# Laced conditioning weights as split single passes, and cache rows transposed behind the queries

## The reference

```
mod = silu(c) @ w_ada + b_ada                 # c: two conditioning vectors of 1024; w_ada: 1024 x 6144
sh1, sc1, gt1, sh2, sc2, gt2 = split(mod, 6)
h = x * (1 + sc1) + sh1
z = h @ w_in                                  # cq, ckv, kr, gu, gv
q = rms(cq) @ w_uq;  ckv = rms(ckv);  kr = rope(kr)        # ckv, kr are outputs too
a = chunk_causal_attention(q, ckv_all @ w_uk + kr_all, ckv_all @ w_uv)
b = gelu(gu) * (W_s LN(gelu(gv)) + b_s)       # gMLP; the normalised v rows of the sample are an output
m = [rms(a) * g_a, rms(b) * g_b] @ w_o
x1 = LN(alpha * x + (1 + gt1) * m);  then a product-key expert layer, and x2 = LN(...)
```

## Time and profile before

| | |
|---|---|
| median of 3 runs | 1888.17 us (1888.16 to 1888.47) |
| the profiled execution | 1888.05 us |
| its span in the profile | 1886.2 us |
| TensorE busy | 1747.3 us (93%) |
| VectorE, ScalarE, GpSimd busy | 1439.2, 672.8, 835.0 us |

### The profile page before, as it was taken

The page is one execution under the profiler, slowest core; times in us unless marked ns, Lnnn a source line. Parts: engine busy times, 40 slices in busy tenths (PEclk is TensorE's granted clock), DMA queues, the critical chain, the costliest instruction groups (busy, mean ns, idle before and its releaser), DMA issues.

```text
span 1886.2 us, 28376 instructions
## 1 busy us (share of the span) xinstructions
PE 1747.3 (93%) x9464; PEld 1501.2 (80%) x9464; DVE 1439.2 (76%) x2852; ACT 672.8 (36%) x948; POOL 835.0 (44%) x633
## 2 busy tenths in 40 slices
PE   7799899999699699898799999999999999999995
PEld 1799753486599599788688989989889899898894
DVE  2532614444599999979299998988999999999997
ACT  1223233322222245578333333333333333333333
POOL 1114210010333256678465555545556555555564
PEclk9899979999799899999899999999999999999997
DMA  8122203322321243544899999999999999999992
GB/s 299 57 68 65 87 27 126 112 90 68 111 68 41 82 157 123 221 155 194 336 389 396 371 380 383 371 379 381 370 371 385 380 382 370 384 379 370 384 341 90
DMA packets 144116, 459.41 MB, mean 244 GB/s; under 512 B 13936, under 2 KB 46720, under 8 KB 143136
## 3 DMA queue, kind: packets, MB, share of 16 engines
q1 hardware_dynamic: 85808, 224.42, 33.8%
q0 software_dynamic: 57360, 208.72, 28.8%
q10 hardware_dynamic: 864, 25.17, 3.2%
HBM read 423.31 MB, written 34.68 MB: 243 GB/s over the span
## 4 chain that ended last, share of the span: by engine, by line
PE 82%; DVE 7%; ACT 4%; DMA 3%; POOL 2%; issue 2%; ACTq 0%; DVEq 0%; POOLq 0%; SPq 0%
PE ps L620 81%; ACT piece L1076 2%; POOL e_lo L569 1%; DMA early_activations<-e_out 1%; DMA g_in<-dense_gates 1%; DMA w_raw<-peer_uT 1%; ACT e_hi L1076 1%; DVE tmp L1433 0%; DMA consts_sb<-consts 0%; POOL act_lo L514 0%; DMA gath<-peer_u,idx 0%; DVE stats L1916 0%; POOL w_lo L507 0%; PE ps L868 0%; DVE y_tok L1914 0%
## 5 line engine op out<-in xcount | busy, mean ns | idle before, releaser
L620 PE MATMUL ps<-act_hi,w_hi 128*128 128x384 f32 (+1 forms) x1496 | 480.4, 321 | 46.4 <-POOL w_lo L507 20.3
L620 PE MATMUL ps<-act_hi,w_lo 128*128 128x384 f32 (+1 forms) x1496 | 475.8, 318 | 0.0
L620 PE MATMUL ps<-act_lo,w_hi 128*128 128x384 f32 (+1 forms) x1496 | 475.3, 318 | 0.0
L602 POOL DMA_INDIRECT gath<-peer_v,idx x192 | 259.2, 1350 | 205.1 <-DVE f_full L1827 159.1
L602 POOL DMA_INDIRECT gath<-peer_u,idx x192 | 251.6, 1311 | 209.6 <-DVE act L1822 175.8
L620 PEld LDWEIGHTS ps<-act_hi,w_hi 128*128 128x128 f32 x1496 | 284.6, 190 | 52.4 <-POOL w_lo L507 20.4
L620 PE MATMUL ps<-v_hi,ga_hi 128*128 128x512 f32 x768 | 299.5, 390 | 3.1 <-DVE v_lo L1811 3.1
L620 PE MATMUL ps<-v_hi,ga_lo 128*128 128x512 f32 x768 | 301.2, 392 | 0.0
L620 PE MATMUL ps<-v_lo,ga_hi 128*128 128x512 f32 x768 | 301.2, 392 | 0.0
L620 PEld LDWEIGHTS ps<-act_lo,w_hi 128*128 128x128 f32 x1496 | 284.5, 190 | 4.2
L620 PEld LDWEIGHTS ps<-act_hi,w_lo 128*128 128x128 f32 x1496 | 284.2, 190 | 0.0
(11 more groups left out here) (268 smaller groups left out, 2725.7 us busy)
## 6 DMA issues: line engine op xcount, KB each, us to landing
w_raw<-peer_uT SPq DMA_DIRECT2D x128, 512.0 KB, 6.9
v_raw<-peer_v SPq DMA_DIRECT2D x96, 512.0 KB, 7.7
w_raw<-ada SPq DMA_DIRECT2D x48, 512.0 KB, 3.5
dense_gates<-piece ACTq DMA_DIRECT2D x6, 4096.0 KB, 11.8
g_in<-dense_gates SPq DMA_DIRECT2D x32, 768.0 KB, 14.3
w_raw<-peer_v SPq DMA_DIRECT2D x32, 512.0 KB, 7.1
w_raw<-w_in SPq DMA_DIRECT2D x17, 512.0 KB, 3.3
w_raw<-w_pq SPq DMA_DIRECT2D x16, 512.0 KB, 3.6
```

What stands on the lines that cost most here:

```text
L602: pool.indirect_dma_start(out=gath[:, u % GB, :], out_offset=None, in_=table, in_offset=bass.IndirectOffsetOnAxis(ap=idx12[:, par, u:u + 1 ...
L620: return nc.tensor.matmul(out, lhsT, rhs, start=start, stop=stop)
```

## The change

The 24 laced slots are split like the other weights: ACT writes the high part of slot x to `w_hi[x % 2]` (`ada_high`), GpSimd the low part to `w_lo[x % 2]` (`ada_low`). The condition is split too, into four columns `silu_hl` (high part of two vectors, low part of two). A piece is then two single passes, `silu_hl` with the high and with the low part of the weights, which sum into four rows of PSUM; VectorE adds the two pairs of columns in `conditioning`. The transposes of the cache rows move from behind the gMLP product to behind the swap of q's rope halves, ahead of w_uk, in banks 2 and 3; `o_tok` moves to the region of the probabilities, and `new_v` is sent behind its DMAs. Four of the eight pieces ahead of the loop move in front of the token sums. The semaphores `vmean` and `vvar` are merged into `rowsA`, which makes room for `ahi` and `alo`. The places of the new buffers:

```
+        silu_hl = at("silu_hl", [P, KD, 4], R["small"] + 1024, F32R)
...
-        o_tok = at("o_tok", [P, NT, KVL + ROPE], R["rows"])
+        o_tok = at("o_tok", [P, NT, KVL + ROPE], R["p"])
...
+        def ada_slot(x):
+            r = RING_AT["ada2"] + x
+            return r % RING, 16 * (r // RING + 1)
+        N_LACED = 4 * len(LACED)
+        A0 = FIRST["ada2"]
```

GpSimd, behind the output DMAs:

```
-            low_mix(0, GH)
+            def ada_low(x):
+                pool.wait_ge(s["ahi"], x + 2)
+                nc.gpsimd.tensor_tensor(w_lo[:, x % 2], w_raw[:, ada_slot(x)[0]], w_hi[:, x % 2].bitcast(F32),
+                                        ALU.subtract).then_inc(s["alo"], 1)
+            for x in range(7):
+                ada_low(x)
+            low_mix(0, 2)
+            for x in range(7, 9):
+                ada_low(x)
+            low_mix(2, GH)
+            for x in range(9, N_LACED):
+                ada_low(x)
```

TensorE: `ada_piece`, then the transposes behind the swap of q's rope halves (the same lines, with banks 6 and 7, are removed from behind the gMLP product), then the order ahead of the units, where the token sums stand behind the wait for `sqb`:

```
                 j, i = divmod(n, 2)
+                x = 4 * (g - LACED[0]) + j
                 if i == 0:
-                    pe.wait_ge(s_w[r % RING], 16 * (r // RING + 1))
-                ins = mm(ps[0:2, 7, :], silu_c[:, n, :], w_raw[:, r % RING, i * 512:(i + 1) * 512], n == 0, n == 7)
+                    pe.wait_ge(s["alo"], x + 1)
+                c = slice(i * 512, (i + 1) * 512)
+                mm(ps[0:4, 7, :], silu_hl[:, n, :], w_hi[:, x % 2, c], n == 0, False)
+                ins = mm(ps[0:4, 7, :], silu_hl[:, n, :], w_lo[:, x % 2, c], False, n == 7)
                 if i == 1:
                     ins.then_inc(s["adaused"], 1)
...
             pe.wait_ge(s["ckvn"], 1)
+            for t, (t0, n) in enumerate(TILES):
+                k0 = t0 if t < SAMPLE else NEW
+                if t >= 2:
+                    pe.wait_ge(s["ote"], t - 1)
+                for c in range(CK):
+                    nc.tensor.transpose(ps[0:n, 2 + t % 2, c * P:(c + 1) * P], ckvT[:, c, k0:k0 + n], ident)
+                nc.tensor.transpose(ps[0:n, 2 + t % 2, KVL:KVL + ROPE], krT[0:ROPE, k0:k0 + n],
+                                    ident[0:ROPE, 0:ROPE]).then_inc(s["otr"], 1)
             pe.wait_ge(s_cache, 32)
             pe.wait_ge(s_ukv, 32)
             KH = KEYS // 2
             for h in range(HEADS):
+                if h == 1:
+                    pe.wait_ge(s["ote"], NT)
...
             scores(0)
+            pe.wait_ge(s["bt"], 4)
+            for n in range(4):
+                ada_piece(LACED[0], n)
+            pe.wait_ge(s["bt"], NT)
             pe.wait_ge(s["sqb"], 1)
...
-            for n in range(8):
+            for n in range(4, 8):
                 ada_piece(LACED[0], n)
```

ACT: at the start, then behind the value rows, behind the first `token_deviations`, and in the units (the waits for the transposes and the copy to `probT` stand between `ada_high(4)` and `mix_high`):

```
+            f(silu_hl[:, :, 0:2], silu_c[:]).then_inc(s["ahi"], 1)
...
+            def ada_high(x):
+                slot, landed = ada_slot(x)
+                act.wait_ge(s_w[slot], landed)
+                act.wait_ge(s["adaused"], A0 + x - 1)
+                f(w_hi[:, x % 2], w_raw[:, slot]).then_inc(s["ahi"], 1)
...
+            act.wait_ge(s["wused"], END["w_uq"])
+            for x in range(2):
+                ada_high(x)
             act.wait_ge(s["bt"], NT)
...
             token_deviations(1)
+            for x in range(2, 4):
+                ada_high(x)
...
+            act.wait_ge(s["out"], 16 * (1 + 2 * NT))
             for i, (h, t) in enumerate(units):
...
                 if i == 0:
                     ada_copy(LACED[0])
+                    ada_high(4)
...
                 if 1 <= i <= GH:
-                    act.wait_ge(s["out"], 16 * (1 + 2 * NT))
                     mix_high(i - 1)
+                if 5 + i < N_LACED:
+                    ada_high(5 + i)
                 if i % 4 == 3:
                     ada_copy(LACED[1 + i // 4])
```

VectorE, in `conditioning`:

```
+                parts = src.rearrange("p (f c) -> p f c", c=rows)
+                ins = v.tensor_tensor(mod[:, f0:f1], parts[:, :, 0:2], b_ada, ALU.add)
+                if rows == 4:
+                    step(ins)
+                    ins = v.tensor_tensor(mod[:, f0:f1], mod[:, f0:f1], parts[:, :, 2:4], ALU.add)
```

More of the change, by code:

```diff
@@ L331, in build @@
         names = """lo_odd silu adaused adaev adat var std xn xT x0e mod h32 hhi hlo whi wlo wused evac sqz rowsA
[L332 removed]
+            ahi alo
+            cqrow vc2 vvarr vn cqn cqhi cqlo ckvn krmm krr qmm qr kmm kev vmm vev vtt vte gmm bt sc
             mx ex pn pt pte pv pve rowsB rowr sqa sqb mhi mlo m mean1 rc1 sq1 var1 varr h2 h2hi h2lo smm h2t
@@ L533, in _ @@
             pool.dma_start(bs[:], a["b_s"].partition_broadcast(P)).then_inc(s_gm, 16)
-            pool.wait_ge(s["vte"], NT)
-            pool.dma_start(a["new_v"], v_tok[0:DEC, SAMPLE, :]).then_inc(s["out"], 16)
             for t, (t0, n) in enumerate(TILES):
@@ L541, in _ @@
                 pool.dma_start(dst_k, o_tok[0:n, t, KVL:]).then_inc(s["out"], 16)
+            pool.wait_ge(s["vte"], NT)
+            pool.dma_start(a["new_v"], v_tok[0:DEC, SAMPLE, :]).then_inc(s["out"], 16)
             def low_mix(i0, i1):
@@ L637, in ada_piece @@
                     wait(pe, s["adaev"], g)
-                part = max((k for k in FIRST if k.startswith("ada") and FIRST[k] <= 4 * g), key=FIRST.get)
                 j, i = divmod(n, 2)
-                r = RING_AT[part] + 4 * g + j - FIRST[part]
+                x = 4 * (g - LACED[0]) + j
                 if i == 0:
-                    pe.wait_ge(s_w[r % RING], 16 * (r // RING + 1))
-                ins = mm(ps[0:2, 7, :], silu_c[:, n, :], w_raw[:, r % RING, i * 512:(i + 1) * 512], n == 0, n == 7)
+                    pe.wait_ge(s["alo"], x + 1)
+                c = slice(i * 512, (i + 1) * 512)
+                mm(ps[0:4, 7, :], silu_hl[:, n, :], w_hi[:, x % 2, c], n == 0, False)
+                ins = mm(ps[0:4, 7, :], silu_hl[:, n, :], w_lo[:, x % 2, c], False, n == 7)
                 if i == 1:
@@ L726, in _ @@
             pe.wait_ge(s["cqrow"], 2)
-            column_sums(6, z, range(Z_GV, Z_GV + GH)).then_inc(s["vmean"], 1)
+            column_sums(6, z, range(Z_GV, Z_GV + GH)).then_inc(s["rowsA"], 1)
             def v_squares():
                 pe.wait_ge(s["vc2"], 1)
-                column_sums(4, tmp, range(GH)).then_inc(s["vvar"], 1)
+                column_sums(4, tmp, range(GH)).then_inc(s["rowsA"], 1)
             def swapped_kr():
@@ L809, in _ @@
             pe.wait_ge(s["vte"], NT)
[L810 to L820, removed]
             def token_sums(c, src, at, begin, end):
@@ L836, in laced_columns @@
             def laced_columns(g):
-                n = 8 * (g - LACED[0])
-                ada_columns(g, ps[:, 6, n:n + 8])
+                n = 16 * (g - LACED[0])
+                pe.wait_ge(s["adaev"], g + 1)
+                for j in range(4):
+                    ins = nc.tensor.transpose(ps[:, 6, n + 4 * j:n + 4 * j + 4], cond[0:4, j * P:(j + 1) * P], ident[0:4, 0:4])
+                ins.then_inc(s["adat"], 1)
             scores(0)
+            pe.wait_ge(s["bt"], 4)
+            for n in range(4):
+                ada_piece(LACED[0], n)
+            pe.wait_ge(s["bt"], NT)
             pe.wait_ge(s["sqb"], 1)
@@ L1079, in _ @@
             f(silu_c[:].rearrange("p k c -> p (k c)"), vecs[:, VEC_AT["c"]:VEC_AT["c"] + 16], ACT.Silu).then_inc(s["silu"], 1)
+            act.wait_ge(s["silu"], 1)
+            f(silu_hl[:, :, 0:2], silu_c[:]).then_inc(s["ahi"], 1)
             def ada_copy(g, bank=7):
+                n = 4 if g in LACED else 2
                 act.wait_ge(s["adaused"], 4 * g + 4)
                 wait(act, s["adat"], g)
-                f(cond[0:2, :], ps[0:2, bank, :]).then_inc(s["adaev"], 1)
+                f(cond[0:n, :], ps[0:n, bank, :]).then_inc(s["adaev"], 1)
+            def ada_high(x):
[3 more added lines that the diff above has]
+                f(w_hi[:, x % 2], w_raw[:, slot]).then_inc(s["ahi"], 1)
             for g in range(ORDER["ada"] // 4):
@@ L1152, in _ @@
             linear("w_uq", qT, at={3: v_deviation})
+            for t, (t0, n) in enumerate(TILES):
+                act.wait_ge(s["otr"], t + 1)
+                f(o_tok[0:n, t, :], ps[0:n, 2 + t % 2, 0:KVL + ROPE]).then_inc(s["ote"], 1)
             for h in range(HEADS):
@@ L1406, in _ @@
                                 ALU.subtract, ALU.mult).then_inc(s["xn"], 1)
+            dve.wait_ge(s["ahi"], 1)
+            v.tensor_tensor(silu_hl[:, :, 2:4], silu_c[:], silu_hl[:, :, 0:2].bitcast(F32), ALU.subtract).then_inc(s["ax"], 1)
             dve.wait_ge(s_vec, 16)
@@ L1414, in _, with conditioning @@
                                 ALU.mult, ALU.add).then_inc(s["x0e"], 1)
-            def conditioning(f0, f1, src):
+            def conditioning(f0, f1, src, rows=2):
                 dve.wait_ge(s["adat"], f1 // 4)
                 b_ada = vecs[:, VEC_AT["b_ada"] + f0:VEC_AT["b_ada"] + f1].unsqueeze(2).to_broadcast([P, f1 - f0, 2])
-                ins = v.tensor_tensor(mod[:, f0:f1], src.rearrange("p (f c) -> p f c", c=2), b_ada, ALU.add)
+                parts = src.rearrange("p (f c) -> p f c", c=rows)
```

(9 more changed lines are left out.)

5 lines of the change are left out of this document (1 added, 4 removed).

## The result

The changed kernel takes 1904.4 us (median of five runs, 1900.99 to 1905.69) against 1888.47 for the kernel before on the same chip: a ratio of 1.0073 over all the runs (the medians alone give 1.0084), 95% interval 1.006 to 1.0085. The forecast was 1898, its range 1887 to 1908; the forecast case's own range, 1892 to 1904, is missed by 0.4. The profiled execution took 1904.84 us; its span is 1903.0 against 1886.2, 16.8 more.

The account below looks back on a forecast made before the run. TensorE was taken to bound the kernel, with no idle time through attention, where the change makes a closed ring. Terms -5.0, +1.3, -3.4, +0.9, +12.1, +1.4, +2.5 sum to +9.8 us on 1888: 1898, range 1887 to 1908.

Parts of the forecast that it names:

- the forecast case: Likeliest case: the ring paces the attention loop, clock mostly held; 1892 to 1904 us, chance 0.62.
- Transposes, -5.0: Cache-row transposes, covered by TensorE's 2.67 us wait before w_uk, cost nothing; ACT's square follows VectorE's product at once: -5.0 us.
- First two splits, +1.3: During the gMLP product, GpSimd's subtracts for slots 0 and 1 slow VectorE: +1.3 us, bounds 0 and twice that.
- Token sums, -3.4: 40 passes of 8.6 us before attention may start at 2.4 GHz: -3.4 us, bounds 0 and -4.3.
- Sums to the loop, +0.9: End of token sums to ACT free after unit 1's mix part: waits for slots 2 and 3 replace pieces, +0.9 us.
- Loop, +12.1 and +2.5 for clock and queue: Attention units 2 to 18: closed ring takes 93.0 us against 80.9, +12.1; clock drops and held tensor_scalars add +2.5.
- End of the loop, +1.4: From unit 18's copy to w_o's high part: 5.9 us instead of 4.4, +1.4 us.
- The sign given in the prediction: In attention, TensorE waits 1.2 to 1.8 us per unit for GpSimd's w_lo, about 18 times.
- Clock lost throughout: Rival: TensorE at 1.2 GHz in more than half of 18 attention units, 9 to 18 us, 1904 to 1914; chance 0.15.
- Hidden: Rival: attention splits ready when TensorE reaches its piece, 3.9 us a unit, about 1868 us; chance 0.10.
- Only a subtract under 1 us would do it: Condition for hidden splits: 3.58 us hand-over must fit TensorE's 2.0; only another ACT order or subtract under 1 us.
- Cancel: Rival: front gains everything (-8), ring 0.2 us a unit shorter (8.7), no clock loss, about 1890 us; chance 0.13.

Follow-up runs that it names:

- The order experiment: Changed kernel with ACT's high part of slot 5+i moved ahead of its wait for unit i's transposes: 1888.93 us, ratio 0.9996.
- The engine experiment: Changed kernel with low parts on VectorE instead of GpSimd, first two high parts early, later ones still behind the copy of probT: 1874.84 us, ratio 0.9918.
- order and engine changed: Changed kernel with high parts ahead of ACT's wait, those of slots 0 and 1 early, and low parts on VectorE: 1870.91 us, ratio 0.9903.

## Why the prediction came out as it did

The mechanism was right: the high part behind probT closes a ring through GpSimd, TensorE's saving turns into waiting, and the loop gets longer. The order experiment shows it by opening the ring: the waits for w_lo go, and 11.8 of the 14.1 us with them. The engine experiment, which also shortens the ring, agrees. Term by term, in the profiled executions:

- *Transposes, -5.0*: the square does follow the product at once, but "they cost nothing" failed. The weights came 2.1 us later, and the clock in w_uk took 1.6 more in this execution: together -1.3. The step that failed is the cover: I checked TensorE's idle time and the banks, not what else happens on the DMA engines in it.
- *First two splits, +1.3*: 2.9 (24.6 against 21.8 us), just above the upper bound of 2.6. I had taken the price for two instructions slowing each other; in fact the held one waits until the subtract ends.
- *Token sums, -3.4*: -3.3 (5.42 for 8.70), at a clock of 0.84.
- *Sums to the loop, +0.9*: -0.1 (19.25 for 19.3). Negmax, for which I had added up to 1.4, wasn't held.
- *Loop, +12.1 and +2.5 for clock and queue*: 14.1 for 14.6 forecast. That the sum came out is in part luck: the parts were off in opposite directions. At the full clock a unit of three blocks ran 5.30 us and one of four 5.42 (high part to high part, 351.20 to 361.92), where I had 5.44 and 5.65. At 1.2 GHz one of one block took 6.11 for 5.01, one of two 6.45 for 5.22 (366.83 to 379.39). The clock over the loop was 0.80, which is some 38 of its 95.1 us at 1.2 GHz. I wrote that most scalings "fall just clear" of a subtract; all twenty fall into one, but end 0.08 to 0.35 us behind it, when TensorE has only just got w_lo as well, so that they cost little.
- *End of the loop, +1.4*: 2.2.

With 0.5 for the pieces in front of the sums this is +15.0 at w_o against +9.8. The cover (3.7) and the first splits (1.6) alone are as much as the difference; the smaller misses cancel. The last 1.8 us lie behind w_o: from its first matmul to the end 1502.8 us, against 1501.0 and 1501.7 in the two profiles of before and 1500.5 to 1503.0 in the other ten. I found no part of the change there and can't tell it from that spread.

The sign given in the prediction held in kind, not in size: TensorE waits for w_lo 18 times, 22.6 us in all (1.26 each), but the count is chance. Five of these waits, the longest (3.9) among them, lie outside the loop; in it 13 of 17 units wait, 0.2 to 2.2 us and 14.3 in all. The four without a wait (pieces at 344.32, 349.74, 371.06, 377.18) lie in stretches at 1.2 GHz or right behind one, where TensorE's own work took as long as the hand-over. Two other signs missed: the square came at 267.66, not near 262, and probT every 5.0 to 7.0 us, not 5.0 to 5.7.

*Rivals.* "Clock lost throughout" didn't come: 0.80 over the loop, not 0.5; but some 38 of 95.1 us at 1.2 GHz is not far below the "more than half" that I priced at 1904 to 1914. "Hidden" was priced at 3.9 us a unit, 14 us off the loop, if the hand-over fitted: with order and engine changed the loop is 13.8 shorter than before. "Only a subtract under 1 us would do it" isn't refuted: with 1.21 and the old order the splits aren't all hidden (74.7, not 67.1), but the loop is already below 80.9. "Cancel" described the order alone (1888.9), for another reason: GpSimd's hold on VectorE, not a front that gained everything.

*Open*: what moves the instruction packet; whether it is the cause of the late weights or goes along with it; ACT's copies without transposes were not tried, nor one-column matmuls in place of the transposes. Counted in TensorE's matmul records from the start, the packet comes at records 1230 to 1238 in twelve profiles and at 1246 in the one with fifteen idle transposes. That would fit a packet of TensorE's own stream, which the moved transposes let run on ahead of its wait for the weights; the thirteenth profile doesn't fit it, so this isn't shown.

## What to carry to other kernels

Where engine A hands a part to B, B to C, and C's result is what A waits for before the next part, the loop can't run faster than the sum of all the hand-overs (5.20 us in the unit shown), however idle each engine is: look in the in-order queue for work that could stand ahead of the wait; the two buffers that w_hi and w_lo have didn't open this ring. A cheaper engine may cost more by what it holds up: 2.35 us on GpSimd held VectorE's small operations, so that ACT waited 15.2 us for negmax (with the early order, 292 to 378 us); 1.21 us on VectorE itself left 4.1 (292 to 360 us). A stretch that is idle on the engine in question isn't free until one has looked at what the DMA engines do in it.

## What the runs showed of the hardware

- Which of VectorE's operations a GpSimd subtract holds when they begin inside it. Held until 0.03 to 0.6 us behind its end: products and squares of two operands in SBUF (2.13 us for 0.69, 2.48 for 0.29) and tensor_scalars from SBUF to SBUF (scaling of probabilities 1.87 for 0.38; five elements 1.27). Not held inside one: row maxima and copies from PSUM, operations with one operand in PSUM (0.68), reciprocals (0.16), memsets (0.11), and negmax, a tensor_scalar on one element (0.15 at 290.72, with 2.2 us of the subtract to go). The Trainium skill, GPSIMD Engine Reference, Key points, speaks of contention for shared interfaces with two SBUF inputs or a two-port mode; the trace agrees in kind and shows its size as the rest of the subtract.
- The granted clock in w_uk was full in four profiles, with waits of 0, 0.9, 1.0 and 2.67 us ahead, and 0.50 for some 3 us at or shortly behind its start in nine, with waits of 1.3 to 2.8; the kernel before did both.
- One packet of instructions (16 KB, 0.95 us of one DMA engine) in the midst of the weights went with 1.2 to 2.4 us of later landing. The Trainium skill, Runtime: NRT & Kernel Launch, Instruction fetch mechanics, says that streams are refilled in blocks of 16 KiB by a DMA queue and that the cost is mostly hidden; the size agrees, and here it may not have been hidden.
